# Differential attention: the sums of squares of q, k and the outputs as two short-form products of split squares in place of one fp32 product

## The reference, cut to what matters

```python
def _rms_norm(x, g=None, eps=1e-6):
    xf = x.astype(jnp.float32)
    y = xf * lax.rsqrt(jnp.mean(xf * xf, axis=-1, keepdims=True) + eps)
    ...

q, k, v = jnp.split(h @ w_in, [2 * A_HEADS * A_HD, 4 * A_HEADS * A_HD], axis=-1)
q = _rms_norm(q.reshape(bsz, t, A_HEADS, 2, A_HD), qk_norm[0])
k = _rms_norm(k.reshape(bsz, t, A_HEADS, 2, A_HD), qk_norm[1])
v = v.reshape(bsz, t, A_HEADS, A_VD)
...
p = jax.nn.softmax(jnp.where(visible, logits, NEG_INF), axis=-1)
pd = p[:, 0] - lam_full * p[:, 1]
...                                   # o = pd @ v for each block of queries
o = _rms_norm(o, subln) * (1.0 - lambda_init)
```

## Time and profile before

| | us |
|---|---|
| median of 3 runs | 1703.96 |
| lowest and highest of them | 1703.01, 1704.0 |
| the profiled execution | 1705.07 |
| its span, first to last instruction | 1703.3 |
| PE busy | 1672.1 (98%) |
| DVE, ACT, POOL busy | 956.5, 835.8, 736.2 |

### The profile page before, as it was taken

The page is one execution under the profiler, slowest core; times in us unless marked ns, Lnnn a source line. Parts: engine busy times, 40 slices in busy tenths (PEclk is TensorE's granted clock), DMA queues, the critical chain, the costliest instruction groups (busy, mean ns, idle before and its releaser), DMA issues.

```text
span 1703.3 us, 34375 instructions
## 1 busy us (share of the span) xinstructions
PE 1672.1 (98%) x13441; PEld 1630.8 (96%) x13441; DVE 956.5 (56%) x1188; ACT 835.8 (49%) x1161; POOL 736.2 (43%) x489
## 2 busy tenths in 40 slices
PE   7999999999999999999999899999999999999999
PEld 6999999999999999999999899999999988899999
DVE  6685555633655556545466745555555567665553
ACT  5444454455544544443466544444444446654442
POOL 6235553354555545553332355533554324245520
PEclk9999999999999999999999999999999999999999
DMA  7658876643887756676643466665667741356673
GB/s 204 174 162 228 233 200 189 166 118 94 217 223 200 205 148 173 173 200 171 176 108 89 111 183 174 189 183 148 173 173 190 184 108 51 100 149 191 179 209 112
DMA packets 538562, 283.55 MB, mean 166 GB/s; under 512 B 12112, under 2 KB 532817, under 8 KB 538481
## 3 DMA queue, kind: packets, MB, share of 16 engines
q1 hardware_dynamic: 538065, 281.30, 60.6%
q0 software_dynamic: 352, 1.09, 0.3%
q10 hardware_dynamic: 64, 0.02, 0.0%
HBM read 281.29 MB, written 5.53 MB: 168 GB/s over the span
## 4 chain that ended last, share of the span: by engine, by line
PE 79%; DVE 7%; ACT 7%; DMA 3%; SPq 1%; issue 1%; POOL 1%; POOLq 0%; ACTq 0%; DVEq 0%
PE bank L1599 24%; PE bank L1601 24%; PE bank L1600 24%; ACT w_hi L702 3%; DVE w_lo L1112 3%; PE bank L1969 2%; ACT al L885 1%; PE bank L1625 1%; DMA raw<-in_w_down 1%; SPq L380 1%; PE bank L1932 1%; DMA raw<-in_ffn_wi 1%; DVE xg_lo L1123 1%; DVE aqkv L1316 1%; DMA raw<-in_a_in 1%
## 5 line engine op out<-in xcount | busy, mean ns | idle before, releaser
L1599 PE MATMUL bank<-xg_hi,w_hi 128*128 128x272 f32 (+1 forms) x2576 | 740.7, 288 | 7.5 <-DVE w_lo L1112 7.5
L1601 PE MATMUL bank<-xg_hi,w_lo 128*128 128x272 f32 (+1 forms) x2576 | 734.6, 285 | 0.0
L1600 PE MATMUL bank<-xg_lo,w_hi 128*128 128x272 f32 (+1 forms) x2576 | 732.8, 284 | 0.0
L1112 DVE TENSOR_TENSOR w_lo<-raw,w_hi 128x2048 fp32r<-128x2048 f32 (+3 forms) x200 | 501.1, 2505 | 260.5 <-ACT w_hi L702 260.2
L702 ACT ACTIVATE w_hi<-raw 128x2048 fp32r<-128x2048 f32 (+3 forms) x212 | 442.0, 2085 | 266.1 <-PE bank L1601 252.7
L1599 PEld LDWEIGHTS bank<-xg_hi,w_hi 128*128 128x128 f32 x2576 | 485.7, 189 | 11.7 <-DVE w_lo L1112 8.5
L1601 PEld LDWEIGHTS bank<-xg_hi,w_lo 128*128 128x128 f32 x2576 | 486.0, 189 | 0.0
L1600 PEld LDWEIGHTS bank<-xg_lo,w_hi 128*128 128x128 f32 x2576 | 484.8, 188 | 0.7
L585 POOL TENSOR_TENSOR up<-gate,up 128x256 f32<-128x256 f32 (+1 forms) x132 | 304.2, 2305 | 257.6 <-ACT gate L1038 257.5
L1599 PE MATMUL bank<-act_hi,w_hi 128*128 128x256 f32 (+1 forms) x1056 | 300.9, 285 | 0.2
L1600 PE MATMUL bank<-act_lo,w_hi 128*128 128x256 f32 (+1 forms) x1056 | 300.7, 285 | 0.0
(11 more groups left out here) (294 smaller groups left out, 1843.8 us busy)
## 6 DMA issues: line engine op xcount, KB each, us to landing
raw<-in_ffn_wi SPq DMA_DIRECT2D x176, 512.0 KB, 4.9
raw<-in_ffn_wo SPq DMA_DIRECT2D x32, 1408.0 KB, 7.2
raw<-in_w_gate SPq DMA_DIRECT2D x44, 512.0 KB, 4.1
raw<-in_w_up SPq DMA_DIRECT2D x44, 512.0 KB, 5.3
raw<-in_w_down SPq DMA_DIRECT2D x16, 1408.0 KB, 7.1
raw<-in_a_w_in SPq DMA_DIRECT2D x24, 512.0 KB, 5.4
raw<-in_a_in SPq DMA_DIRECT2D x20, 512.0 KB, 6.4
raw<-in_w_o SPq DMA_DIRECT2D x16, 512.0 KB, 4.9
```

Of the source, the lines that this page charges most:

```text
L1112: v.tensor_tensor(w_lo[slot][:, 0:n], raw[slot][:, 0:n], w_hi[slot][:, 0:n].bitcast(F32), ALU.subtract).then_inc(rest_ready, 1)
L1599: mm(to, lhsT=w_hi[slot][:, w], rhs=hi[:, k, cols], start=start and i == 0, stop=False)
L1600: mm(to, lhsT=w_hi[slot][:, w], rhs=lo[:, k, cols], start=False, stop=False)
L1601: ins = mm(to, lhsT=w_lo[slot][:, w], rhs=hi[:, k, cols], start=False, stop=stop and i == len(order) - 1)
```

## The change

The squares of q and k are split as the weights are: ACT writes the squares `asq` in fp32, waits for them, and copies them to `asq_hi` (short form). POOL subtracts, `asq_lo = asq - asq_hi`, in a new step `low_squares`. PE sums `asq_hi` and `asq_lo` into the same bank by `halves_r`, a short-form copy of `halves`. The outputs' squares get the same in heads 0 to 5 (`osq_hi`, `osq_lo`, `low_outputs`, `ones_r`). In heads 6 and 7 the outputs' sum stays one fp32 product.

In PE's order `out_sums` of a head moves from the end of a pass to the next pass, behind part 0 and ahead of `sums`. POOL's new steps stand behind the weight split of each chunk. POOL makes `halves_r` and `ones_r` at the start.

```diff
@@ POOL, start
+            gp.tensor_copy(halves_r[:, :], halves[:, :])
+            gp.tensor_copy(ones_r[:, :], ones[:, :])
@@ POOL, diff
+            def low_squares(i):
+                gp.wait_ge(a_sq_hi, i + 1)
+                if i:
+                    gp.wait_ge(a_sums, i)
+                gp.tensor_tensor(asq_lo[:, :, :], asq[:, :, :], asq_hi[:, :, :].bitcast(F32), ALU.subtract).then_inc(a_sq, 1)
+            def low_outputs(b):
+                gp.wait_ge(a_osq_hi, b + 1)
+                if b:
+                    gp.wait_ge(a_osum, b)
+                gp.tensor_tensor(osq_lo[:, :], osq[:, :], osq_hi[:, :].bitcast(F32), ALU.subtract).then_inc(a_osq, 1)
+            low_squares(0)
             for c in range(2, 8):
...
                 split(g, 2 * n, 3 * n).then_inc(rest_ready, 1)
+                if c >= 3:
+                    low_outputs(c - 3)
+                low_squares(c - 1)
+            low_outputs(5)
+            low_squares(7)
@@ ACT, diff_mixer
                         act.wait_ge(a_o, b + 1)
-                        act.activation(osq[:, :], bank[:, 5, 0:TOK], ACT.Square).then_inc(a_osq, 1)
+                        if b:
+                            act.wait_ge(a_osq, b)
+                        squares = act.activation(osq[:, :], bank[:, 5, 0:TOK], ACT.Square)
+                        if b < 6:
+                            settle(squares)
+                            act.activation(osq_hi[:, :], osq[:, :], ACT.Copy).then_inc(a_osq_hi, 1)
+                        else:
+                            squares.then_inc(a_osq, 1)
...
                         act.wait_ge(parts_read, 2 * mixer_order(st["diff"], i) + 2)
-                        act.activation(asq[:, :, :], aqkv[:, i % 2, 0:2, :], ACT.Square).then_inc(a_sq, 1)
+                        if i:
+                            act.wait_ge(a_sq, i)
+                        settle(act.activation(asq[:, :, :], aqkv[:, i % 2, 0:2, :], ACT.Square))
+                        act.activation(asq_hi[:, :, :], asq[:, :, :], ACT.Copy).then_inc(a_sq_hi, 1)
@@ PE, sums
-                        ins = mm(bank[:, 6 + m, 0:TOK], lhsT=halves[:, :], rhs=asq[:, m, :], start=True, stop=True)
+                        mm(bank[:, 6 + m, 0:TOK], lhsT=halves_r[:, :], rhs=asq_hi[:, m, :], start=True, stop=False)
+                        ins = mm(bank[:, 6 + m, 0:TOK], lhsT=halves_r[:, :], rhs=asq_lo[:, m, :], start=False, stop=True)
@@ PE, out_sums
-                    mm(bank[:, 3, 0:TOK], lhsT=ones[:, :], rhs=osq[:, :], start=True, stop=True).then_inc(a_osum, 1)
+                    if h >= 6:
+                        mm(bank[:, 3, 0:TOK], lhsT=ones[:, :], rhs=osq[:, :], start=True, stop=True).then_inc(a_osum, 1)
+                        return
+                    mm(bank[:, 3, 0:TOK], lhsT=ones_r[:, :], rhs=osq_hi[:, :], start=True, stop=False)
+                    mm(bank[:, 3, 0:TOK], lhsT=ones_r[:, :], rhs=osq_lo[:, :], start=False, stop=True).then_inc(a_osum, 1)
@@ PE, diff_mixer
-                    _, _, _, turn_probs, outputs, out_sums = steps[i - 2] if i > 1 else [None] * 6
-                    for step in (lambda: part(0), sums, lambda: part(1), turn_probs,
-                                 lambda: part(2, range(4)), logits, turn_values, outputs, lambda: part(2, range(4, KT)), out_sums):
+                    _, _, _, turn_probs, outputs, _ = steps[i - 2] if i > 1 else [None] * 6
+                    out_sums = steps[i - 3][5] if i > 2 else None
+                    for step in (lambda: part(0), out_sums, sums, lambda: part(1), turn_probs,
+                                 lambda: part(2, range(4)), logits, turn_values, outputs, lambda: part(2, range(4, KT))):
...
                 early(2, 0, range(5))
+                steps[5][5]()
                 sums()
```

More of the change, by code:

```diff
@@ L127, in two_blocks @@
         ident, ones, halves, tri = (sb(n, [P, P]) for n in ("ident", "ones", "halves", "tri"))
+        halves_r, ones_r = sb("halves_r", [P, P], F32R), sb("ones_r", [P, P], F32R)
         eps, gains, small = sb("eps", [P, 1]), sb("gains", [P, P + KT]), sb("small", [P, 4])
@@ L162, in two_blocks @@
             aqkv = sb("aqkv", [P, 2, 3, TOK], F32, ph)
+            asq_hi, asq_lo = (sb(n, [P, 2, TOK], F32R, ph) for n in ("asq_hi", "asq_lo"))
+            osq_hi, osq_lo = (sb(n, [P, TOK], F32R, ph) for n in ("osq_hi", "osq_lo"))
             asq, aln, avn = sb("asq", [P, 2, TOK], F32, ph), sb("aln", [P, 2, TOK], F32, ph), sb("avn", [P, 3, P], F32, ph)
@@ L230, in two_blocks @@
         a_logits, a_max, a_exp, a_pd, a_turned, a_pt = (sem(n) for n in ("a_logits", "a_max", "a_exp", "a_pd", "a_turned", "a_pt"))
+        a_sq_hi, a_osq_hi = sem("a_sq_hi"), sem("a_osq_hi")
         a_o, a_osq, a_osum, a_orms, a_oy = (sem(n) for n in ("a_o", "a_osq", "a_osum", "a_orms", "a_oy"))
```

## The result

The changed kernel takes 1708.91 us (median of 9 runs, 1708.41 to 1713.02) against 1703.96 for the kernel before: ratio 1.0034, 95% interval 1.0025 to 1.0043. It is slower by 4.95 us, beyond the 0.2% that can be told from no change. The forecast was 1708.4.

The account below looks back on a forecast made before the run. The prediction took a DVE and ACT loop, not PE, to bound the stage: -0.41 us on PE plus 4.83 for ACT's copies gave +4.4, so 1703.96 became 1708.4 us (forecast 1707.4 to 1709.5, range 1703.5 to 1712.0).

Parts of the forecast that it names:

- What bounds the kernel: Differential-attention stage: a closed loop over DVE and ACT, 14.19 us a head, sets the pace; PE's own work about 13.7.
- the pairs: DVE's two L1316 steps per head, normalising q and k; middle heads' were to come 14.9 us apart instead of 14.19.
- Part 1: Shorter products on PE save 4.5 us, but only one head's 0.41 us, at the start, lies on the path.
- Part 2: ACT's copies of the q and k squares add 0.69 us in each of seven heads, 4.83 us in all.
- Part 3: ACT's copies of the output squares, at most 0.45 us each, cost nothing; 0.05 to 0.40 us of idle cover left.
- Part 4: POOL's subtractions land just in time; ACT's wait on the moved output sum costs nothing, with 0.1 to 0.4 us room.
- E: End of an L1316 pair on DVE (871.06 us in the profile before), from which the forecast measured later events.
- Sum: Whole kernel: -0.41 + 4.83 = +4.4 us, the whole shift going to the end, median 1708.4 us.
- a fourth thing: The granted clock falling as PE idles more, above all around head 7: 1 to 3 us, counted with the late-subtraction rival.
- rival C: A subtraction or the output sum comes late in the heads: 1709.5 to 1714 us; chance 0.13 with the clock.
- A: Rival: PE sets the pace, so the shorter products' whole gain comes through, 1699.4 us; chance 0.15.
- B: Rival: the copy costs the loop less, perhaps by less POOL split overlap on L1316, 1704.5 to 1707.4 us; chance 0.14.

Follow-up runs that it names:

- e1: Kernel before, with q and k squares written in short form and summed by one short-form product, low half left out: 1702.99 us, ratio 0.9991.
- e2: Kernel before, with only ACT's wait and short-form copy of the q and k squares added, read by nobody: 1708.64 us, ratio 1.0025.
- e6: Kernel before, with POOL's split of the second weight part put behind DVE's first tile: 1701.49 us, ratio 0.9982.
- e8: Changed kernel's q and k part alone, ACT writing the high half directly, POOL squaring and subtracting, its second weight split later: 1701.21 us, 0.9981 of the kernel before.
- e3: Changed kernel with q and k squares back in one fp32 product; outputs' split and moved sum kept: 1705.28 us, 1.0007 of the kernel before.
- e5: Changed kernel, but ACT writes the high half directly from q and k and POOL makes the fp32 square: 1705.02 us, 1.0004 of the kernel before.
- e7: Changed kernel with POOL's second weight part, subtractions, then third part, all behind DVE's first tile: 1704.48 us, 0.9999 of the kernel before.

## Why the prediction was right, point by point

**What bounds the kernel.** Right, and e1 and e2 are the proof: 5.3 us off PE gave 1.8 us (3.1 at the edge of the interval) and left the pairs where they were, 0.7 us a head onto ACT gave the whole shift. The Trainium skill (Perfetto Trace Analysis, Identifying the Most-Contended Engine) would have TensorE improved first; the runs disagree for this stage, as long as the loop is 14.19 and PE's work 13.77 us.

**Part 1.** -0.41 us at the start, measured -0.40 at the first pair. The other 4.1 us went into PE's waits, which the longer loop lengthened further: 7.6 us at the logits and 2.3 at the sums, 1.8 of them in head 7. The price of 0.41 us a head came out again between e6 and e8 (13.77 to 13.35).

**Part 2.** 0.69 us a head forecast, 0.70 measured between squares and exponentials, 0.65 to 0.72 in the pairs of heads 1 to 7, 4.79 in seven. e2 gives the same with nothing else changed.

**Part 3.** Cost nothing that shows, as forecast: 0.38 us of the cover is left in a middle head, where 0.85 - 0.45 = 0.40 was expected. At the tightest place 0.05 was expected and none is left (the squares at 860.39 have no wait before them), and that pair is 0.71 us further from the one before it, hardly more than the others.

**Part 4.** The subtractions take 1.36 and 0.79 us (1.36 and 0.7 to 0.8 forecast). The low half of q and k is there at 878.06, 7.2 us after the end of the pair at 870.88, as forecast. PE stands 1.77 us at the sums of head 7 (2 forecast), and 1.6 in heads 3 to 5 at the logits (1.8 forecast; 0.6 to 1.3 in the others that wait). The output sum holds nobody up in heads 1 to 6, also as forecast. But the step had more in it than I saw. I called the room 0.1 to 0.4 us and the price nothing. The figures held it (the sum at E + 7.6, ACT at E + 7.36 without the 0.69), but I did not draw from them that the room exists only because the copy delays ACT. e3 and e5 take the copy away, and the moved sum costs 0.19 us a head.

**Sum.** +4.4 us forecast up to head 7, +4.39 measured. What followed was not in the sum: 1.6 us of a fall of the clock behind head 7 (in the prediction as a fourth thing, 1 to 3 us, with rival C), 1.2 earlier at the start of the mixer and 1.0 less in the rest, where the fall of the kernel before at 1401 is missing. The kernel before shows a fall of the same kind in both of its profiles. That the two falls nearly cancel in this pair of profiles is luck. In the medians +4.95 stand against the +4.4, which lies near the lower edge of the interval of the ratio (+4.3 to +7.3 us); the 0.5 us between them are about what the lower mean clock of the changed kernel's runs would cost (an estimate from the runs above: 2.1 us for 0.004, so 0.5 for 0.001).

**The rivals.** A is out: pairs farther apart, no PE pieces in the chain of the middle heads, and e1. B did not occur: L1352 is held as before, up to 1516 ns:

```profile
L1352 DVE SCALAR_TENSOR_TENSOR aqkv<-aqkv,small,aln x16: 487/494/1516, 839.9 to 941.0; 128x272 f32<-128x272 f32 x16
```

Its mechanism is real, though, and larger than I had weighed it: e6 and e7 took 1.0 us a head out of the loop by it. The Trainium skill (GPSIMD Engine Reference, 1. Specifications) says that GpSimd's SBUF interfaces are shared with VectorE, with contention for VectorE instructions of two SBUF inputs. The traces agree, with 1519 ns under a split and at most 503 without. C as a late subtraction did not occur: the subtractions fall where DVE is idle, and though PE waited for them in heads 1 and 7 (0.6 and 1.8 us), the pairs and the probabilities of head 7 came no later for it. Its price was too low by its own terms, though: seven heads at 1.36 us on top of the 4.4 would be 1717.9, not 1714.

## What to carry to other kernels

Where an engine is busy for 98% and still waits once in every round, find the loop that releases it before making its work shorter, and price each added instruction by whether it stands in that loop: here 4.5 us off TensorE were worth 0.4, and 0.7 us a head on ScalarE cost all of itself. Shorten the loop first (here by moving a GpSimd split off a VectorE instruction, 3 us), and only then does the shorter product come through in the pace (0.41 us a head in the traces; the medians could not tell it). When a step is moved into a gap, ask whether the gap is there only because of another part of the same change.

## What the runs showed of the hardware

- A GpSimd split of 128x1024 held the VectorE instruction L1316 (two SBUF inputs) until it ended: 1519 ns instead of 496 in the kernel before, at most 503 in e6. One 128x3 step was held as well: 1.65 us in e8, with the split over it ending at 891.66 and the step at 891.69, against 0.23 us in the kernel before.
- TensorE's granted clock fell to 1.2 GHz for about 3.4 us at places that changed from one execution to the next of the same kernel (949 or 1401 in the kernel before; 953, or 902, 940, 953 and 1407 in the changed one). On the path such a fall cost 1.1 us (in a middle head, at 902) to 1.6 us (behind head 7).
